# Four U rows in flight for block 2, gathers from block 0's first head on, and another order of taps, gates and output gate

## The reference

```python
h = rmsnorm(x); P = h @ W_in                    # q k v, output gate, decays, GLU, two branch gates
yA = (rmsnorm(gla(q, k, v, decays)) * silu(og)) @ w_o
yB = silu(layernorm(conv31(a_in * sigmoid(a_gate)) + b)) @ w_pw2
x = x + (sigmoid(gA) * yA + sigmoid(gB) * yB) @ w_out
h2 = rmsnorm(x)
q = h2 @ w_q                                    # PEER, per token and for each of 8 heads:
s = q . keys; two top-16 of 128, then top-16 of the 256 sums -> 16 expert numbers, softmax gates
act = gelu(u_tab[idx] . h2); x = x + sum((gate * act) * v_tab[idx])
out = rmsnorm(x)
```

## Time and profile before

| | |
|---|---|
| median of 3 runs | 4772.74 us (4771.23 to 4778.17) |
| profiled execution | 4765.59 us, span 4763.9 us |
| busy | PE 3783.1 (79%), DVE 2743.7 (58%), POOL 1339.6 (28%), ACT 873.1 us (18%) |
| moved | 1530.72 MB, 1073.81 of it by gathers |
| first dot; step 130's merge; block 3's first dot | 1303.9; 2456.8; 4095.8 us |

### The profile page before, as it was taken

One profiled execution on the slowest core, in us unless ns is written; L12 is line 12 of the kernel. 1 busy time (PEld: TensorE's weight loads), 2 busy tenths in 40 slices (PEclk: granted clock), 3 DMA queues, 4 the chain that ended last, 5 costly groups with the idle time before them and its releaser, 6 DMA issues. The chain is left out here.

```text
span 4763.9 us, 44159 instructions
## 1 busy us (share of the span) xinstructions
PE 3783.1 (79%) x15280; PEld 2399.6 (50%) x15280; DVE 2743.7 (58%) x3996; ACT 873.1 (18%) x2035; POOL 1339.6 (28%) x1038
## 2 busy tenths in 40 slices
PE   6999999999999999766679798510788876777776
PEld 3444469996755576762668685310334432223232
DVE  1332249000599987866677777778665565455444
ACT  1322220100111111241111111111111211212111
POOL 0000000000022221323454444455333333344443
PEclk9999999999999999888889899755899999999999
DMA  2111126677588888999999999999999999999998
GB/s 102 54 70 53 53 106 264 251 273 277 212 336 352 346 363 329 414 407 407 418 388 426 396 426 418 380 360 341 359 372 367 378 357 372 383 420 421 415 417 367
DMA packets 194520, 1530.72 MB, mean 321 GB/s; under 512 B 24279, under 2 KB 30551, under 8 KB 30809
## 3 DMA queue, kind: packets, MB, share of 16 engines
q0 software_dynamic: 147456, 1073.81, 56.3%
q1 hardware_dynamic: 45232, 444.87, 23.6%
q10 hardware_dynamic: 1740, 10.91, 0.6%
HBM read 1525.32 MB, written 4.19 MB: 321 GB/s over the span
## 5 line engine op out<-in xcount | busy, mean ns | idle before, releaser
L582 POOL DMA_INDIRECT arena_c<-in_peer_u,arena_c x384 | 539.4, 1405 | 2904.3 <-DVE arena_c L1301 1563.2
L1301 DVE SCALAR_TENSOR_TENSOR arena_c<-arena_c 128x2048 f32<-128x2048 f32 x384 | 878.8, 2289 | 590.8 <-DMA arena_c<-in_peer_u,arena_c 584.6
L1624 PE MATMUL bank<-arena_h,wring 128*128 128x384 f32 (+3 forms) x3200 | 887.9, 440 | 25.6 <-ACT arena_h L727 9.0
L586 POOL DMA_INDIRECT arena_c<-in_peer_v,arena_c x512 | 643.4, 1257 | 423.5 <-DVE arena_h L1528 171.7
L1728 PE MATMUL bank<-arena_h,wring 128*128 128x128 f32 (+2 forms) x4608 | 660.6, 305 | 100.0 <-DVE arena_h L1380 52.5
L1624 PEld LDWEIGHTS bank<-arena_h,wring 128*128 128x128 f32 x3200 | 542.8, 197 | 367.1 <-issue 160.3
L1728 PEld LDWEIGHTS bank<-arena_h,wring 128*128 128x128 f32 x4608 | 617.0, 193 | 146.1 <-issue 81.8
L1936 PE MATMUL bank<-arena_c,arena_h 128*128 128x512 f32 x1024 | 504.8, 641 | 170.9 <-ACT arena_h L886 150.6
L1970 PE MATMUL bank<-arena_c 128*128 128x512 f32 x1024 | 485.4, 623 | 173.2 <-ACT arena_c L930 162.7
L1311 DVE SCALAR_TENSOR_TENSOR arena_o<-arena_c,arena_o 128x2048 f32<-128x2048 f32 x256 | 600.7, 2346 | 7.1 <-ACT arena_c L765 4.6
L763 ACT ACTIVATE arena_c<-arena_c 128x1 f32<-128x1 f32 x384 | 77.9, 203 | 2206.1 <-DVE arena_c L1301 2206.0
(11 more groups left out here) (214 smaller groups left out, 2558.8 us busy)
## 6 DMA issues: line engine op xcount, KB each, us to landing
wring<-in_w_in SPq DMA_DIRECT2D x112, 2048.0 KB, 8.2
wring<-in_gla_w_o SPq DMA_DIRECT2D x24, 2048.0 KB, 9.9
wring<-in_conv_w_pw SPq DMA_DIRECT2D x24, 2048.0 KB, 11.1
wring<-in_w_out SPq DMA_DIRECT2D x24, 2048.0 KB, 13.5
wring<-in_peer_w_q SPq DMA_DIRECT2D x24, 2048.0 KB, 11.0
arena_c<-in_peer_v,arena_c POOLq DMA_INDIRECT x512, 11.4
arena_c<-in_peer_u,arena_c POOLq DMA_INDIRECT x384, 8.4
arena_c<-in_x SPq DMA_DIRECT2D x4, 1024.0 KB, 12.6
```

The costliest lines, as they stand in the source:

```text
L582: pool.indirect_dma_start(out=u_rows[s], out_offset=None, in_=u_tab[0], in_offset=at)\
L586: pool.indirect_dma_start(out=v_rows[s], out_offset=None, in_=v_tab[0], in_offset=at)\
L1301: V.scalar_tensor_tensor(row, row, 1.0, block_of(h2, b), ALU.mult, ALU.mult, accum_out=act_u[:, k:k + 1]).then_inc(u_used, 1)
L1624: last = M(ps[bank][:, 0:hi - lo], w_slot(slot)[:, k, m * P:m * P + P], act_in[:, k, lo:hi], start=k == 0, stop=k == KT - 1)
```

## The change

- Block 2 has four U rows in flight (`u3_row`: two in arena_h, two where blocks 0 and 1 had theirs). Its gathers use block 3's semaphores. `diag1`, the scores, block 2 and 3's h2T and some work areas move to other places for it.
- Block 0's heads are selected one by one: heads 0 and 1 ahead of step 0, heads 2 to 7 beside steps 0 to 5. The first expert numbers are copied, and so released to POOL, after head 0. ACT copies out heads 4 to 7 beside steps 0 and 1.
- A glu1 turn is now three slabs (gate, value, block 1's gate of branch B). The first is taken at step 8. Its taps are on block 1 alone (128 wide, steps 8 to 59); the values of blocks 2 and 3 are kept in `cv`, and their taps (256 wide, `fill`) follow in steps 53 to 104, out of a padded copy of two tiles.
- The output gate follows the turns (steps 58 to 79), then ma1 (81 to 88), pw (91 to 94), w_out (96 to 100). Block 1's LayerNorm is done at steps 62 to 67, that of blocks 2 and 3 at steps 115 to 131.
- Block 1's queries are read out one head a step (105 to 112) instead of every second step.
- The final gain is loaded at step 9 of block 3 instead of ahead of it. Several semaphores are merged.

The core of the diff:

```diff
-TURN_AT = (0, 10, 20, 30, 40, 47, 54, 61, 68)
-OG_AT = (4, 7)
-IT_AT = (2, 4)
-X1_AT = 67
-GB_AT = 66
-XC_AT, SQUARE_AT = 71, 72
-RSTD_AT, ROOT_AT, RECIP_AT = 77, 77, 78
-SCALE1_AT, SILU1_AT = 79, 80
-PW_AT = 83
-SCALE2_AT, SILU2_AT = 84, 85
-RES1_AT = (93, 95, 97, 99)
-NORM1_AT = 100
+TURN_AT = (8, 15, 21, 28, 34, 41, 47, 54, 60)
+GB_LATER = 3
+OG_AT = tuple(range(58, 82, 3))
+XC1_AT, RSTD1_AT, RECIP1_AT, SCALE1_AT = 62, 65, 66, 67
+IT_AT = tuple(range(81, 89))
+X1_AT = 89
+PW_AT = 91
+GAIN1_AT = 95
+RES1_AT = (96, 97, 99, 100)
+NORM1_AT = 101
 QUERY1_AT = 105
+
+FILL = ((53, 0), (78, 70), (86, 250), (95, 420), (104, 8 * 63))
+XC2_AT, RSTD2_AT, RECIP2_AT, SCALE2_AT = 115, 121, 122, 123
...
-        s_0 = view(arena_c, RU, 2, PH, NK)
+        s_0 = view(arena_c, MG, 2, PH, NK)
...
+        diag1 = view(arena_c, MG + 1536, VS, P)
+
+
+        u3_row = [view(arena_h, 0, D), view(arena_h, D, D), view(arena_c, RU, D), view(arena_c, RU + D, D)]
...
+            with sp.Fori(0, PH // 2) as i:
+                for j in range(2):
+                    for at, (w, o) in enumerate(((w_in, WGATE), (w_in, WGLU), (w_in, WGB))):
+                        load(SB_GLU1 + 3 * j + at, i, 6, slot_all((3 * j + at) % 2), slab(w, i * 2 + (o + j)))
+            slab_loads(SB_OG1, w_in, WOG)
+            pair_loads(SB_MA1, w_in, WGA, w_o, 0)
...
-            gathers(SIDE // 2, idx_ready, idx_cur, u_row, u_ready, u_used, v_row, v_ready, v_used)
-            gathers((UNITS - SIDE) // 2, idx2_ready, idx_cur2, u2_row, u2_ready, u2_used, v2_row, v2_ready, v2_used)
+            gathers(PH, idx_ready, idx_cur, u_row, u_ready, u_used, 0, v_row, v_ready, v_used, 0)
+            gathers(PH // 2, idx_ready, idx_cur, u3_row, u2_ready, u2_used, 0, v_row, v_ready, v_used, STEPS, 2 * PH)
+            gathers(PH // 2, idx2_ready, idx_cur2, u2_row, u2_ready, u2_used, PH * TOP, v2_row, v2_ready, v2_used, 0)
...
+            def queries0(h):
+                queries_out(h, h % 2, 1, qh0)
+                scores_out(h, h % 2, 1, lambda c: s_0[:, c, h:h + 1, :])
+
+            for h in range(2):
+                queries0(h)
+                exponentials(h, 1, work_0)
+            queries0(2)
+            queries0(3)
...
+                if s == 0:
+                    queries0(4)
+                    exponentials(2, 1, work_0)
+                    queries0(5)
+                if s == 1:
+                    queries0(6)
+                    exponentials(3, 1, work_0)
+                    queries0(7)
+                if 2 <= s < 6:
+                    exponentials(s + 2, 1, work_0)
...
-                    V.tensor_tensor(upad1[:, m, PAD:PAD + T1], ps[2 + m][:, 0:T1], sig1[:, m, :], ALU.mult)\
+                    chain.mark(V.tensor_tensor(upad1[:, m, PAD:PAD + GL], ps[2 + m][:, 0:GL], sig1[:, m, 0:GL], ALU.mult))
+                    V.tensor_tensor(cv[:, 2 * j + m, 2 * P:T], ps[2 + m][:, P:T1], sig1[:, m, P:T1], ALU.mult)\
                         .then_inc(p["use"], 1)
                 chain.wait()
-                dve.wait_ge(p["use"], 2 * j + 4)
-
-            def conv1(j, first, end):
+                chain.step(V.tensor_copy(kept, upad1[:, :, PAD + KEEP:PAD + P]))
...
+            def fill(first, end):
 
                 for n in range(first, end):
-                    r, m = n // 2, n % 2
-                    dst = cv[:, 2 * j + m, P:T]
-                    tap = cols[:, 2 * j + m, R_CW + r:R_CW + r + 1]
-                    if r == 0:
-                        ins = V.tensor_scalar(dst, upad1[:, m, 0:T1], tap, cols[:, 2 * j + m, R_CB:R_CB + 1],
-                                              ALU.mult, ALU.add)
+                    j, at = n // 63, n % 63
+                    if at:
+                        taps(j, at - 1, at, upad2, 2 * P, T, cv_done)
                     else:
-                        chain.wait(but=1)
-                        ins = V.scalar_tensor_tensor(dst, upad1[:, m, r:r + T1], tap, dst, ALU.mult, ALU.add)
-                    if r < TAPS - 1:
-                        chain.mark(ins)
-                    else:
-                        ins.then_inc(cv1_done, 1)
-
-                        chain.wait()
-
-            def og1_scale(j, s):
+                        if j:
+                            dve.wait_ge(cv_done, 2 * KT + 2 * j)
+                        else:
+                            chain.step(V.memset(upad2[:, :, PAD + T2:], 0.0))
+                            dve.wait_ge(pair["glu1"]["use"], 2 + KT)
+                        chain.mark(V.tensor_copy(upad2[:, :, 0:PAD], u_keep[:, 2 * j:2 * j + 2, :]))
+                        chain.step(V.tensor_copy(upad2[:, :, PAD:PAD + T2], cv[:, 2 * j:2 * j + 2, 2 * P:T]))
...
+                if s < PH - 2:
+                    find, softmax = topk_0(s + 2)
+                    all_of(find)
+                    softmax()
...
+                if s in IT_AT:
+                    ma1_merge(IT_AT.index(s))
+                if 0 <= s - PW_AT < 4:
+                    mb1_merge(2 * (s - PW_AT))
+                    mb1_merge(2 * (s - PW_AT) + 1)
+                if s <= FILL[-1][0]:
+                    fill(filled(s - 1), filled(s))
...
+                if s == NORM2_AT + 4:
+                    dve.wait_ge(n2_h, 4)
+                    dve.sem_inc(u2_used, SLOTS - US)
...
+            for h in range(2):
+                find, softmax = topk_0(h)
+                all_of(find)
+                if h == 0:
+                    V.tensor_copy(idx_cur[:, 0, :], idx_all[:, 0, :]).then_inc(idx_ready, 1)
+                softmax()
...
-                    dot(U, b, k)
+                    s = k % SLOTS
+                    dve.wait_ge(u2_ready[s], (U - 2 * PH) * (16 * TOP // SLOTS) + 16 * (k // SLOTS + 1))
+                    row = by_tile(u3_row[s])
+                    V.scalar_tensor_tensor(row, row, 1.0, block_of(h2, b), ALU.mult, ALU.mult,
+                                           accum_out=act_u[:, k:k + 1]).then_inc(u2_used, 1)
...
-            dve.wait_ge(v_used, 2 * PH * TOP + VS)
+            dve.wait_ge(u_used, STEPS + US)
+            dve.sem_inc(u2_used, US)
+            dve.wait_ge(v_used, STEPS + VS)
...
+                slab_ready(first + 2, i, per)
+                pe.wait_ge(pair["mb1"]["sig"], i * 2 + (m0 + 1))
+                tiles(slot, hT, 4 + m0, P, 2 * P, pair["mb1"]["gate"])
...
-            glu1(SB_GLU1, 0, 2, 0, 0)
-            with pe.Fori(0, 4) as j:
-                for s in range(2):
-                    slab_ready(SB_OG1 + s, j, 4)
-                    for m in range(2):
-                        pe.wait_ge(og1["used"], j * 4 + (2 * s + m + 1))
-                        project(s, m, hT, 4 + 2 * s + m, og1["mm"], P, T)
-                    slab_used()
-                glu1(SB_OG1 + 2, j, 4, 1, j)
+            with pe.Fori(0, PH // 2) as i:
+                for m in range(2):
+                    glu1(SB_GLU1 + 3 * m, i, 6, m)
+
+            def og1_slab(n):
+                slab_ready(SB_OG1 + n)
+                for m in range(2):
+                    pe.wait_ge(og1["used"], 2 * n + m + 1)
+                    project(n % 2, m, hT, 4 + 2 * (n % 2) + m, og1["mm"], P, T)
+                slab_used()
+
+            def ln_mean(ln, lo, hi):
+                for t in range(KT):
+                    last = M(ps[0][:, 0:hi - lo], ones_d[:], cv[:, t, lo:hi], start=t == 0, stop=t == KT - 1)
+                last.then_inc(ln["sum"], 1)
+
+            pe.wait_ge(pair["mb1"]["sig"], 2 + 8)
+            og1_slab(0)
+            og1_slab(1)
+            pe.wait_ge(pair["glu1"]["use"], 2 + KT)
+            pe.wait_ge(cv_done, 2 * KT)
+            ln_mean(ln1, P, 2 * P)
+            og1_slab(2)
+            for t in range(KT):
+                pe.wait_ge(ln1["sq"], t // 2 + 1)
+                M(ps[1][:, 0:P], ones_d[:], sqr1[:, t // 2 % 3, t % 2, :], start=t == 0, stop=t == KT - 1)\
+                    .then_inc(ln1["sq_used"], 1)
+            for n in range(3, 8):
+                og1_slab(n)
             pe.wait_ge(og1["used"], 4 + KT)
-            with pe.Fori(0, 3) as j:
+            with pe.Fori(0, PH // 2) as i:
                 for a in range(2):
-                    ma1(SB_MA1 + 2 * a, j, 6, a, j * 2 + (a + 1))
-                glu1(SB_MA1 + 4, j, 6, 5, j)
-            for a in range(2):
-                ma1(SB_MA1_LAST + 2 * a, 0, 4, a, 6 + a + 1)
-
-            def mb1_gate(n):
-                slab_ready(SB_GB1 + n)
-                if n >= 4:
-                    pe.wait_ge(pair["mb1"]["sig"], n - 3)
-                tiles(n % 2, hT, 4 + n % 4, P, 2 * P, pair["mb1"]["gate"])
-                slab_used()
-
+                    ma1(SB_MA1 + 2 * a, i, 4, a, i * 2 + (a + 1))
```

397 lines of the change are left out of this document (197 added, 200 removed).

## The result

The changed kernel takes 4725.14 us, the median of four runs (4716.12 to 4735.71); the kernel before took 4775.45 beside it (4771.23 to 4791.29). The ratio is 0.9884, with a 95% interval of 0.9861 to 0.9908: faster by 1.2% (the quotient of the two medians alone is 0.9895). The prediction was 4691. The profiled execution took 4721.85 us with a span of 4720.1. One execution further down, of block 2's part alone, took 5022.59 us at a mean granted clock of 0.81 where the others had 0.925 to 0.928, a slower state of the chip, and is left out.

A forecast was written before the change was run, and what follows sets the result against it. It took DMA as near full from a quarter of the span on, elsewhere VectorE, TensorE's slab chain or two U rows in flight. Gains 72 + 10 = 82 gave 4683.6 profiled, 4691 for the median; range 4632 to 4745.

The forecast's parts named there:

- Part 1: Block 2: four U rows in flight make the transfer rate bind, 5.07 us a step; gain 72 us, bounds 55 to 82.
- Part 2: Block 0's start: gathers from the first head on, dot 0 at 1238 instead of 1303.9, 66 us earlier.
- Steps 0 and 1 then cost 12.6 each and steps 2 to 5 14.9 each: Block 0's first steps, one head selected in each: step 6 at 1323, step 8 about 1337, first take at 1339.
- index 0 is ready at 1224: Block 0's selection: about 10 us a head, so the first expert number is there at 1224, its row 8 us later.
- Part 3: New order along TensorE's slab chain up to step 130, at 2445; with the early start 10 us gained, bounds -40 to 57.
- seven turns: The glu1 turns after the first take: 53.4 us each from slab work plus a landing of 10.8, reaching 1702 after six.
- out, norm2 turn: w_out's slabs and block 1's second norm: 21 us a pair to 2214, then 18 plus 6 for fill taps, 2238.
- output gate: landing 11: Output gate after the turns: a landing of 11, eight slabs of 21, LayerNorm sums about 10, last scale 2: ends 1893.
- PE holds two result banks and stands until 2077: At pw: its first merge is at step 91, three steps of 12 after step 88, so TensorE waits until 2077.
- slower: slab landings: Rival, chance 0.07: slabs land in 14.4 us everywhere instead of 10.8, costing 100 us: 4791; sign decided from 13.7.
- the first half loses what it gains: Rival, chance 0.17: holds in ACT and steps bunched with heads, priced as landings of 12.2: -30 instead of +10, 4731.
- holds in ACT: ScalarE's queue: LayerNorm squares wait for TensorE between two slabs, and the experts behind them wait too.

The follow-up runs named there:

- block 2's part alone: The kernel before with four U rows in flight in block 2 and the views moved for it, old order kept: 4700.94 us, ratio 0.9832; again 0.9837.
- the four edits: Changed kernel with output gate's first slab in free banks, pw's merges and glu takes earlier, fill taps moved; together 4684.77 us, ratio 0.9803; again 0.9808.
- pw's merges: The changed kernel with the merges of pw starting at step 89 instead of 91: 4725.98 us, ratio 0.9888.
- the takes: The changed kernel with glu takes at steps 6, 13, 20, 27 instead of 8, 15, 21, 28: 4724.64 us, ratio 0.9893.
- the fill taps' move: The changed kernel with fill taps at 29 a step in steps 79 to 88 and 6.5 a step behind: 4720.56 us, ratio 0.9891.

## Why the prediction came out as it did

The sign and the range were right, the likeliest value was 34 us too low (4691 against 4725.14). Of the two terms of the sum, 72 for block 2 and 10 for the rest, the first was right (78 measured) and the second had the wrong sign (31 lost up to step 256). The sign of the whole came out right by part 1 alone; the order that most of the prediction is about lost time.

**Part 1.** Predicted 72 us, 669 to 688 for the block; measured 674 in the changed kernel and 676 alone, a gain of 78 and 75. Its mechanism, rows in flight, is shown by the kernel with two of them: 759 us. The rate is 408 GB/s (over 400, predicted), the dots' wait 175.9 us (190 predicted); the landings are 11.0 to 11.4, not 12 or more, so four rows never came near their own bound: by the prediction's formula that is (2.3 + 1.4 + 11.4)/4 = 3.8 us a step, an estimate, and a step took 674/128 = 5.3. The rule that spoke against this part would have given no gain: by the Trainium skill's page "DMA: Bandwidth & Descriptors", section "Where 436 GB/s comes from", the HBM side binds at about 358. The trace disagrees: 408 in block 2 and 420 in block 3.

**Part 2, the early start.** The steps "Steps 0 and 1 then cost 12.6 each and steps 2 to 5 14.9 each" and "index 0 is ready at 1224" were too early by 14.4 us at the first take: 1353.4 instead of 1339. Dot 0 comes 4 us late (the first query already starts 6 us later than in the earlier trace rows, on the same code ahead of it). Steps 2 to 5 are 14.9 each, as summed, and what follows up to the take is 3.5 shorter. The miss is in steps 0 and 1, which take 39.4 us instead of 25.2, 11.9 of them the two waits for an exponential behind other heads' copies in ScalarE's queue. The prediction called ScalarE "idle most of the time" and costed its added work at nothing; it is idle, and late all the same, because it stands in order behind a wait for TensorE. That this wait is what delays the first take follows from the rows; its removal alone was not tried. What the early start is worth in the end was not stated as a number in the prediction; the kernel without it shows 15 to 24 us.

**Part 3, TensorE's chain.** Term by term, from the starts of the rows above:

| term | predicted | after | difference |
|---|---|---|---|
| first take | 1339 | 1353.4 | +14 |
| seven turns | 363 | 365.0 | +2 |
| to the first output-gate slab | 11 | 28.1 | +17 |
| output gate | 180 | 182.6 | +3 |
| ma1 | 148 | 154.3 | +6 |
| pw | 89 | 92.1 | +3 |
| out, norm2 turn | 108 | 105.3 | -3 |
| block 1 turned | 2238 | 2280.8 | +43 |
| from there to step 130 | 207 | 205.0 | -2 |

The step that failed is "output gate: landing 11". It took the weights' landing for what ends last there. The code has another wait in front, for the last of eight sigmoids, which ScalarE runs at step 57. The prediction looked for its waits on VectorE and the DMA, and put the sigmoid (0.38 us) at nothing: it did not count its place in a queue whose previous entry waits for VectorE's dot. With free banks for that slab TensorE waits 4.94 us for its weights, the term is 12.6 us instead of 28.1, and the kernel is 21 us faster.

The hold before pw was foreseen ("PE holds two result banks and stands until 2077"): with the shift of 42 us that the chain had by then, 2119 is where it ended, 2119.71. The turns at 52 to 53 us, and landings of 11.3 in the turns, 8.5 to 10.4 in ma1 and 11.4 in out, are as assumed or shorter. ma1 took 6 us more in spite of that: five of its sixteen slabs, each behind a stand of 3.0 to 5.1 us, took 9.04 to 10.19 us instead of the 7.4 counted for each, 9.3 us in all. In the one of 10.19 the granted clock is 0.50 from 1949 to 1955, the lower of its two levels (1.2 GHz), and 1.00 after it. The prediction has no term for this, though the earlier trace rows has 9.18 for the slab behind the 28.95. The term "out, norm2 turn" hides two misses: w_out took 77.5 us (2175.52 to 2252.99) instead of 84, and the norm2 turn behind it 27.8 instead of the 18 and 6 counted, since 28 taps, 11.3 us, lie in its steps. The rival "slower: slab landings" is refuted: no kind of slab here lands in over 11.4 us by its median, and its price began at 13.7. The rival "the first half loses what it gains" (-30 at step 130, 4731) is the one that happened in its amount, and its mechanism in part: its "holds in ACT" were named, at the LayerNorm's squares, and priced through landings; two of the holds were in ScalarE, but at the sigmoid and the exponentials, and longer landings were no part of it.

Some sums of the prediction are off by little and change nothing: eight queries in 1203.6 to 1272.3 are 8.6 us each, not 8.4; 16 slabs at 9.4 are 150, not 148; the taps by its own figures are 68 us more, not 65.

**What stays open.** The amounts of the single edits. The ratios give 0, 0, 0 and 21 us for the four edits alone and 36 to 39 together (0.9884 to 0.9808 and 0.9803); the medians, each against the kernel before beside it, give 1, 3, 8 and 25 alone and 42 to 43 together, which is nearly a plain sum. The interval of one ratio is some 0.4% wide, 9 to 11 us to either side, so a gain of up to about 14 us for an edit alone is not excluded (an estimate from two such intervals). That the gain of one waits for the others is therefore not shown by the times. The rows show it for pw's merges (21.18 gone, 18.35 come, step 130 where it was) and in part for the takes (longer landings). The stand before the norm2 turn, the longest of the chain, was touched by the fill taps' move alone (27.81 to 24.25).
